# A hybrid decoder step: the recurrence's decays move into their own head's step, and four norms share one stretch of logarithms

## The reference

```python
h = rms_norm(x, norm_mix)
z = h @ w_in                            # 2048 -> 7 blocks of 8 heads x 128
q_a, k_a, v_a, q_r, f_r, i_r, g_r = split(z)
q_a = rotary(rms_norm(q_a, q_gain)); k_a = rotary(rms_norm(k_a, k_gain))
o_att = attend(q_a, k_a, v_a, lam)      # softmax of map 1 - lam * softmax of map 2
o_att = rms_norm(o_att, att_gain) * (1 - lam_init)
log_f = log(lb + (1 - lb) * sigmoid(f_r))          # the recurrence's decays
k_r = (1 - lb) * sigmoid(-f_r)
# per step t: S = exp(log_f[t]) * S + k_r[t] v[t];  o[t] = q_r[t] S
o_rnn, state = hgrn2_recurrence(q_r, k_r, i_r, log_f, state0)
o_rnn = rms_norm(o_rnn, rnn_gain) * silu(g_r)
x = x + concat([o_att, o_rnn]) @ w_out
```

## Time and profile before

| | us |
|---|---|
| median of 3 runs | 2925.33 (2924.01 to 2927.54) |
| the profiled execution | 2924.42 |
| its span (first to last record) | 2922.6 |
| around the span | 1.8 |
| a loop round by the windows, clock 1.00 | 113.41 |
| the same, clock 0.99 | 115.04 |

### The profile page before, as it was taken

The page is one execution under the profiler, slowest core; times in us unless marked ns, Lnnn a source line. Parts: engine busy times, 40 slices in busy tenths (PEclk is TensorE's granted clock), DMA queues, the critical chain, the costliest instruction groups (busy, mean ns, idle before and its releaser), DMA issues.

```text
span 2922.6 us, 53276 instructions
## 1 busy us (share of the span) xinstructions
PE 2859.9 (98%) x19979; PEld 2640.6 (90%) x19979; DVE 1502.3 (51%) x2459; ACT 1068.3 (37%) x1481; POOL 97.8 (3%) x75
## 2 busy tenths in 40 slices
PE   6999999999999999999999999999999999999998
PEld 5988888888888898999999999999999999998998
DVE  5455555554554645445554445544455444555454
ACT  4455455455464434222332222332223322234322
POOL 2011010010110100000000000000000000000000
PEclk8999999999999999999999999999999999999999
DMA  5333334333434532333233332333323333232332
GB/s 194 95 109 114 92 92 118 100 98 102 115 102 141 149 97 81 87 93 89 84 93 95 93 89 86 92 94 93 92 80 94 95 93 93 85 90 85 103 106 86
DMA packets 546619, 291.46 MB, mean 100 GB/s; under 512 B 15209, under 2 KB 537571, under 8 KB 546507
## 3 DMA queue, kind: packets, MB, share of 16 engines
q1 hardware_dynamic: 515482, 268.56, 31.5%
q10 hardware_dynamic: 31040, 21.46, 2.3%
HBM read 268.50 MB, written 21.63 MB: 99 GB/s over the span
## 4 chain that ended last, share of the span: by engine, by line
PE 92%; DVE 4%; ACT 2%; issue 2%; SPq 0%; DMA 0%; DVEq 0%; ACTq 0%
PE product L900 27%; PE product L904 14%; PE product L902 14%; PE product L901 14%; PE product L903 13%; PE scratch L707 2%; PE scratch L715 2%; PE scratch L756 1%; PE scratch L809 1%; DVE w_lo L1446 1%; ACT L1074 1%; DVE r_km L1659 1%; DVE act L1683 1%; PE scratch L795 1%; PE scratch L706 1%
## 5 line engine op out<-in xcount | busy, mean ns | idle before, releaser
L900 PE MATMUL product<-act,w_hi 128*128 128x512 f32 x2816 | 1150.9, 409 | 37.2 <-DVE act L1683 14.1
L1446 DVE TENSOR_TENSOR w_lo<-w_raw,w_hi 128x1024 fp32r<-128x1024 f32 (+1 forms) x496 | 607.8, 1226 | 556.7 <-ACT w_hi L1063 556.6
L1063 ACT ACTIVATE w_hi<-w_raw 128x1024 fp32r<-128x1024 f32 (+1 forms) x496 | 514.3, 1037 | 974.8 <-PE product L904 953.0
L904 PE MATMUL product<-act,w_lo 128*128 128x264 f32 x2816 | 807.8, 287 | 0.0
L902 PE MATMUL product<-act,w_hi 128*128 128x264 f32 x2816 | 803.2, 285 | 0.0
L901 PE MATMUL product<-act,w_hi 128*128 128x264 f32 x2816 | 801.9, 285 | 0.0
L903 PE MATMUL product<-act,w_lo 128*128 128x256 f32 x2816 | 794.2, 282 | 0.0
L902 PEld LDWEIGHTS product<-act,w_hi 128*128 128x128 f32 x2816 | 532.5, 189 | 128.6
L900 PEld LDWEIGHTS product<-act,w_hi 128*128 128x128 f32 x2816 | 535.3, 190 | 55.8 <-issue 23.8
L901 PEld LDWEIGHTS product<-act,w_hi 128*128 128x128 f32 x2816 | 535.2, 190 | 3.4 <-issue 1.9
L904 PEld LDWEIGHTS product<-act,w_lo 128*128 128x128 f32 x2816 | 534.4, 190 | 0.0
(11 more groups left out here) (249 smaller groups left out, 2459.4 us busy)
## 6 DMA issues: line engine op xcount, KB each, us to landing
w_raw<-in_w_in SPq DMA_DIRECT2D x112, 512.0 KB, 3.8
w_raw<-in_w_gate SPq DMA_DIRECT2D x88, 512.0 KB, 3.8
w_raw<-in_w_up SPq DMA_DIRECT2D x88, 512.0 KB, 3.8
w_raw<-in_w_down SPq DMA_DIRECT2D x64, 384.0 KB, 3.4
w_raw<-in_w_down SPq DMA_DIRECT2D x64, 320.0 KB, 3.2
w_raw<-in_w_out SPq DMA_DIRECT2D x32, 512.0 KB, 3.9
w_raw<-in_w_ple_gate SPq DMA_DIRECT2D x32, 384.0 KB, 3.4
k_pages<-in_cache_k SPq DMA_DIRECT2D x128, 64.0 KB, 2.8
```

Source lines behind the costliest of these rows:

```text
L900: pe.matmul(both, hi, x[:, k, :, 0:TA], start=begin, stop=False)
L904: mm = pe.matmul(far, lo, x[:, k, 1, TA:T], start=False, stop=end)
L1063: act.activation(w_hi[:, slot, 0:n, :], w_raw[:, slot, 0:n, :], ACT.Copy).then_inc(w_hi_ready, 1)
L1446: dve.tensor_tensor(flat(w_lo[:, slot, 0:n, :]), flat(w_raw[:, slot, 0:n, :]), flat(w_hi[:, slot, 0:n, :]).bitcast(F32), ALU.subtract).the ...
```

## The change

It rewrites the tables of slots. In the loop, the recurrence of head r moves up: `i_nat` 3 to 0, `kh_nat` 7 to 1, `upd` 9 to 2, `intra` 11 to 4, `rnn` 14 to 6, `s_upd` 16 to 7, `s_rnn` 18 to 8, `ssq_r` 20 to 11, and `ssq_a` of head r comes as a task of slot 11 of the next round, where it was slot 27 of its own. `ssq_q` moves from 6 to 10, `rot_q` from 8 to 13, `rot_k` from 12 to 14, `pages0` and `pages1` one slot earlier, `v_nat` from 14 to 15, `score0` from 15 to 16, `att_out` from 25 to 27. The tail has a table of its own.

```diff
 ATTENTION = {
-    6: ["ssq_q"], 8: ["rot_q"], 10: ["ssq_k"],
-    12: ["rot_k"], 13: ["pages0"], 14: ["pages1", "v_nat"], 15: ["k_nat", "score0"],
-    16: ["s_score"], 17: ["score1"], 18: ["w0"], 19: ["s_prob", "score2", "w1"],
-    21: ["score3"], 22: ["w2"], 24: ["w3", "s_out"], 25: ["s_turn", "att_out"], 27: ["ssq_a"],
+    10: ["ssq_q", "ssq_k"], 12: ["pages0"], 13: ["pages1", "rot_q"], 14: ["rot_k"], 15: ["v_nat", "k_nat"],
+    16: ["score0", "s_score"], 17: ["score1"], 18: ["w0"], 19: ["s_prob", "score2", "w1"],
+    21: ["score3"], 22: ["w2"], 24: ["w3", "s_out"], 25: ["s_turn"], 27: ["att_out"],
 }
 RECURRENCE = {
-    3: ["i_nat"], 7: ["kh_nat"], 9: ["upd"], 11: ["intra"], 14: ["rnn"], 16: ["s_upd"], 18: ["s_rnn"], 20: ["ssq_r"],
+    0: ["i_nat"], 1: ["kh_nat"], 2: ["upd"], 4: ["intra"], 6: ["rnn"], 7: ["s_upd"], 8: ["s_rnn"], 11: ["ssq_r", "ssq_a"],
+}
+RECURRENCE_ALONE = {
+    0: ["ssq_a", "i_nat", "kh_nat", "upd"], 4: ["intra"], 6: ["rnn"], 8: ["s_upd"], 10: ["s_rnn"], 12: ["ssq_r"],
 }
 HALVES = 2 * HEAD_CHUNKS
 
-K_PAGES_AT = {True: {10: range(NPG)}, False: {6: range(0, 6), 8: range(6, 11), 10: range(11, NPG)}}
+K_PAGES_AT = {True: {10: range(NPG)}, False: {4: range(0, 6), 6: range(6, 11), 8: range(11, NPG)}}
 V_PAGES_AT = {18: range(0, 6), 20: range(6, 11), 22: range(11, NPG)}
```

```diff
+        SUMS = {"ssq_q": (rr, DK, "rr_q"), "ssq_k": (sq, DK, "rr_k"), "ssq_a": (mix_a, P, "rr_a"), "ssq_r": (mix_r, P, "rr_r")}
+
+        def log_sum(name, it):
+
+            dst, count, _ = SUMS[name]
+            b = take(name, it)
+            func(two(dst[:, :]), m_wide(b), ACT.Ln, scale=1.0 / count, bias=K("eps")).then_inc(free[b], 1)
+
+        def inv_root(name, it):
+
+            dst, _, sig = SUMS[name]
+            act.wait_ge(*read(name, it))
+            func(dst[:, :], dst[:, :], ACT.Exp, scale=-0.5).then_inc(flag(sig), 1)
...
-                    func(sq[:, :], z_k[:, :], ACT.Square).then_inc(flag("sq_k"), 1)
-                if h is not None and s == 10:
+                    func(sq_k[:, :], z_k[:, :], ACT.Square).then_inc(flag("sq_k"), 1)
+                if h is not None and s == 12:
+
+                    beside = ["ssq_r", "ssq_a"] if r is not None else []
+                    for name in beside:
+                        log_sum(name, it)
+                    for name in ["ssq_q", "ssq_k"] + beside:
+                        inv_root(name, it)
+                if h is not None and s == 14:
```

```diff
+                if h is not None and s == 23:
+
+                    act.wait_ge(*evacuated("f", h))
                     func(r_k[:, :], z_f[:, :], ACT.Sigmoid, scale=-1.0)
                     func(z_f[:, :], z_f[:, :], ACT.Sigmoid).then_inc(flag("sig_f"), 1)
+                if r is not None and s == (23 if h is not None else 14):
+
+                    act.wait_ge(flag("r_normed"), r + 1)
                     act.wait_ge(*evacuated("g", r))
-                    func(r_g[:, :], z_g[:, :], ACT.Sigmoid).then_inc(flag("sig_g"), 1)
-                    act.wait_ge(flag("f_done"), r + 1)
+                    func(mix_r[:, :], z_g[:, :], ACT.Sigmoid).then_inc(flag("sig_g"), 1)
+                if h is not None and s == 23:
+                    act.wait_ge(flag("f_done"), h + 1)
                     func(r_kh[:, :], z_f[:, 0:SEQ], ACT.Ln).then_inc(flag("log_f"), 1)
-                if r is not None and s == 2:
-                    act.wait_ge(flag("b_left"), r + 1)
+                if h is not None and s == 25:
+                    act.wait_ge(flag("b_left"), h + 1)
                     func(r_kh[:, :], r_kh[:, :], ACT.Exp).then_inc(flag("exp_left"), 1)
-                    act.wait_ge(flag("b_mid"), r + 1)
+                    act.wait_ge(flag("b_mid"), h + 1)
                     func(r_qm[:, :], r_qm[:, :], ACT.Exp).then_inc(flag("exp_mid"), 1)
-                if r is not None and s == 4:
-                    act.wait_ge(flag("mid_b"), r * SUBS + SUBS)
+                if h is not None and s == 26:
+                    act.wait_ge(flag("mid_b"), h * SUBS + SUBS)
                     for i in range(SUBS):
                         func(r_km(i), r_km(i), ACT.Exp).then_inc(flag("exp_km"), 1)
                     func(r_e[:, :], r_b[:, :], ACT.Exp).then_inc(flag("exp_b"), 1)
@@ -1234,28 +1227,39 @@
...
+                if h is not None and s == 23:
+                    dve.wait_ge(flag("sig_f"), h + 1)
+                    dve.tensor_scalar(z_f[:, :], z_f[:, :], oml[:, bass.ds(h, 1)], lb[:, bass.ds(h, 1)], ALU.mult, ALU.add).then_inc(flag("f_done"), 1)
+                    dve.wait_ge(flag("f_done"), h + 1)
 
                     dve.tensor_copy(f_s[:, :], z_f[:, SEQ:T]).then_inc(flag("f_s_done"), 1)
-                    dve.tensor_scalar(r_k[:, :], r_k[:, :], oml[:, bass.ds(r, 1)], None, ALU.mult).then_inc(flag("r_k_done"), 1)
-                    dve.wait_ge(flag("sig_g"), r + 1)
-                    dve.tensor_tensor(z_g[:, :], z_g[:, :], r_g[:, :], ALU.mult).then_inc(flag("r_gate"), 1)
-
-                    dve.wait_ge(flag("log_f"), r + 1)
+                    dve.tensor_scalar(r_k[:, :], r_k[:, :], oml[:, bass.ds(h, 1)], None, ALU.mult).then_inc(flag("r_k_done"), 1)
+                if h is not None and s == 24:
+                    dve.wait_ge(flag("log_f"), h + 1)
                     for j in range(BLOCKS_T):
                         t = slice(j * P, (j + 1) * P)
                         scan = dve.tensor_tensor_scan(r_b[:, t], K("ones"), r_kh[:, t], 0.0, ALU.mult, ALU.add)
                     scan.then_inc(flag("scan_done"), 1)
-                    dve.wait_ge(flag("scan_done"), r + 1)
+                    dve.wait_ge(flag("scan_done"), h + 1)
                     rb = r_b[:, :].rearrange("p (c t) -> p c t", t=P)
                     dve.tensor_tensor(r_kh[:, :].rearrange("p (c t) -> p c t", t=P),
                                       rb[:, :, P - 1:P].broadcast_to([P, BLOCKS_T, P]), rb, ALU.subtract).then_inc(flag("b_left"), 1)
...
+            pool.wait_ge(flag("exp_left"), h + 1)
+            pool.wait_ge(flag("r_k_done"), h + 1)
             nc.gpsimd.tensor_tensor(r_kh[:, :], r_k[:, 0:SEQ], r_kh[:, :], ALU.mult).then_inc(flag("r_kh_done"), 1)
-            pool.wait_ge(flag("exp_mid"), r + 1)
-            nc.gpsimd.tensor_tensor(r_qm[:, :], z_r[:, 0:SEQ], r_qm[:, :], ALU.mult).then_inc(flag("r_qm_done"), 1)
             rk = r_k[:, 0:SEQ].rearrange("p (c t) -> p c t", t=P)
             for i in range(SUBS):
                 w = (i + 1) * SUB
-                pool.wait_ge(flag("exp_km"), r * SUBS + (i + 1))
+                pool.wait_ge(flag("exp_km"), h * SUBS + (i + 1))
                 t = nc.gpsimd.tensor_tensor(r_km(i), r_km(i), rk[:, :, 0:w], ALU.mult)
             t.then_inc(flag("r_km_done"), 1)
-            pool.wait_ge(flag("exp_b"), r + 1)
-            pool.wait_ge(flag("r_qm_done"), r + 1)
+            pool.wait_ge(flag("exp_mid"), h + 1)
+            pool.wait_ge(flag("exp_b"), h + 1)
+            pool.wait_ge(*evacuated("r", h))
+            nc.gpsimd.tensor_tensor(r_qm[:, :], z_r[:, 0:SEQ], r_qm[:, :], ALU.mult).then_inc(flag("r_qm_done"), 1)
+            pool.wait_ge(flag("r_qm_done"), h + 1)
             nc.gpsimd.tensor_tensor(r_qd, z_r[:, 0:SEQ], r_e[:, :], ALU.mult).then_inc(flag("r_qd_done"), 1)
```

```diff
+                if s == (10 if r is None else 4):
                     if r is None:
 
                         sp.wait_ge(flag("xT_written"), 16)
@@ -567,7 +571,8 @@
                         sp.wait_ge(flag("sq_sum_done"), SUM_EARLY)
                     else:
 
-                        sp.wait_ge(flag("mix_a_done"), h)
+                        sp.wait_ge(flag("sq_a"), h)
+                        sp.dma_start(s_state[:, :, :], a["state_rnn"][0, :, bass.ds(r, 1), :, :].rearrange("b h k v -> k (b h) v")).then_inc(flag("s_state_in"), 16)
...
-                dve.wait_ge(flag("rr_a"), n)
-                dve.scalar_tensor_tensor(mix_a[:, :], oT[:, :], gain_a[:, 0:1], rr[:, :], ALU.mult, ALU.mult).then_inc(flag("mix_a_done"), 1)
+            elif name == "norm_a":
+                dve.wait_ge(flag("rr_a"), m)
+                dve.scalar_tensor_tensor(mix_a[:, :], oT[:, :], gain_a[:, 0:1], mix_a[:, :], ALU.mult, ALU.mult).then_inc(flag("mix_a_done"), 1)
...
+            elif name == "gate_r":
+                dve.wait_ge(flag("sig_g"), m)
+                dve.tensor_tensor(z_g[:, :], z_g[:, :], mix_r[:, :], ALU.mult).then_inc(flag("r_gate"), 1)
                 dve.wait_ge(flag("r_gate"), m)
                 dve.tensor_tensor(mix_r[:, :], r_o[:, :], z_g[:, :], ALU.mult).then_inc(flag("mix_r_done"), 1)
...
+                if h is not None and s == 12:
+                    small("norm_q", it, h, r)
+                    small("norm_k", it, h, r)
+                if r is not None and s == 12:
+                    small("norm_r", it, h, r)
+                if r is not None and h is not None and s == 12:
+                    small("norm_a", it, h, r)
```

(20 more changed lines are left out.)

99 lines of the change are left out of this document (33 added, 66 removed).

## The result

| | before | after |
|---|---|---|
| median, us | 2925.33 (2924.01 to 2930.38) | 2944.07 (2941.03 to 2951.98) |
| profiled execution, us | 2924.42 | 2944.07 |
| its span | 2922.6 | 2942.3 |

The changed kernel is slower: ratio 1.0065, 95% interval 1.005 to 1.0081. The prediction said 2925.7 in a range of 2914 to 2934, so the time lies outside it, and the outcome that it called most likely, no change, did not come.

A forecast was written before the change was run, and what follows sets the result against it. PE, busy 98% of the span, was taken to bound the kernel. The terms -11.7 + 5.5 + 5.0 + 1.1 + 0.5 = +0.4 us gave 2924.8 for the profiled execution, a median of 2925.7 us, range 2914 to 2934.

The forecast's parts named there:

- no change: The forecast and its neighbours, within 0.2% (5.9 us) of the kernel before; chance 0.45.
- Part 1: Front of the round: PE's wait for `w_lo` at slot 4 goes in seven rounds, -11.7 us.
- Part 2: `score0` behind `low`: a new PE wait in all eight heads, +5.5 us, bounds 0 to 13.6.
- A: PE's wait at `score2` of slot 19 until `w0` is read from its scratch buffer, 0.7 us a head.
- Part 3: Decays ahead of chunk 13: a new PE wait in seven rounds, none in head 0, +5.0 us, bounds 0 and 13.3.
- B: PE's wait at slot 26 for the split of chunk 13 (`w_lo`), 0.7 us in each of seven rounds.
- Part 4: Norms at slot 12: ACT's and DVE's work is covered ahead of `rot_q`; cost 0, within about 1 us of showing.
- Part 5: Boundaries: loop entry +1.1 us, the return kept at 0.54 us seven times, the tail +0.5 us.
- The tail: After the loop: half the `act` wait and the `w_lo` wait go, `upd` waits about 3.5 us; +0.5 us, bounds -2 and +3.
- 0.54 is the return itself: At the loop's return: of PE's 0.79 us idle, 0.25 is the evacuation, 0.54 the return, kept seven times.
- Slow: Rival: B is 1.9 us instead of 0.7, ACT and DVE waiting for each other, 2934.1 us; chance 0.17 for B, 0.22 in all.
- Fast: Rival: A and B don't show, 2915.2 us, with one 2920.5; a covered return hole gives 3.8 us more; chance 0.33.

The follow-up runs named there:

- Experiment 2: The changed kernel with PE's seven rounds written out one after the other, other engines keeping their loops: 2928.84 us, ratio 1.0007.
- 4: The changed kernel with two more 128x260 matmuls, result unused, on PE behind `att_out` in all eight heads: 2949.12 us, ratio 1.0076.
- experiment 6: The kernel before with the seven rounds written out on PE alone: 2925.51 us, ratio 0.9998.
- 11: The kernel before with `intra` in two halves, behind the products of slots 11 and 12: 2926.28 us, ratio 1.0006.
- experiment 1: The changed kernel with `att_out` back at slot 25, so PE's round again ends with a product: 2936.16 us, ratio 1.0037.
- 3: The changed kernel with `intra`'s 32 small matmuls in two halves, behind the products of slots 4 and 5: 2939.11 us, ratio 1.0042.
- experiment 5: The changed kernel with PE's seven rounds written out and `intra` in two halves: 2920.79 us, ratio 0.9981 to the kernel before.
- 8: The changed kernel with only `v_nat` back at slot 14 and the gate behind slot 24's scan, its write at slot 25: 2936.7 us, ratio 1.0034.

## Why the prediction was wrong

**Right.** Part 1: slot 4's waits went, 11.7 us in all. Part 2: A predicted at 0.7 us a head, measured 0.76 (6.0 for 5.5). Part 3: B predicted at 0.7 in seven rounds and none in head 0, measured 0.72 (5.0 for 5.0). Its load is 1.28 us and nothing more; had it been the 2.66 of the Trainium skill, "ScalarE: Activation LUTs", "What ACT_TABLE_LOAD costs", B would have been 2.1. Part 4: no wait at `rot_q`. Part 5: the entry +1.1 for +1.1. The tail +1.2 for +0.5 is in its bounds, but partly by luck: the waits for `act` were to halve and went from 4.6 to 4.1 only, and the wait ahead of `upd` was to be 3.5 us and was 2.6. The terms named there (half of `act`, all of `w_lo`, 3.5) give +0.3 and not +0.5.

**Wrong, first: the return, in part 5.** "0.54 is the return itself, and I keep it seven times" took a remainder for a price (and there are six returns, not seven). The price is the branch, 3.3 to 3.9 us from its issue, and what PE has queued then hides it; the branch's row was in the trace of before and not read. The change put `att_out`, 20 short matmul instructions, last on PE's list, where four long ones of `ssq_a` behind a product had been, and the part that shows rose from between 0.8 and 1.2 us to between 1.5 and 2.1: +5.5 us. Of this, 4.8 is the shorter cover (0.8 us less at each return), and the rest is that the six branches took 0.7 us longer in all. Experiment 2 shows the branch as cause, and 4 that what is queued counts by its number of instructions: longer ones in the same places hide more, added ones push the branch's issue back. Experiments 6 and 11 show a second fault of the same step: before, that hole wasn't a cost of its own. It and slot 4's wait came to 2.5 us together, whatever their shares. The change took away the chain, and with it what hid the branch. The Trainium skill, "Runtime: NRT & Kernel Launch", "Instruction fetch mechanics", says that a taken branch whose target isn't among the current two pages waits until its instructions are fetched. The traces give 3.4 to 3.6 us (medians) for the branch and not 0.54. No row shows the fetch itself, and whether the second hole of experiment 1 belongs to it isn't shown.

**Wrong, second: the clock.** The prediction took slow stretches as drift, "it comes and goes without the work changing", 1.7 us either way. Here they follow the work for the greater part: seven in seven rounds, all behind `intra`, where before it was two, one of them behind `intra`. In the rounds that is 5 x 1.7 = 8.5 of +9.7 us, and in the tail two more, 3.4 us. It isn't one execution's bad luck: the mean granted clock is 0.984 to 0.988 in all five runs of the changed kernel, and 0.989 to 0.992 in 14 runs of the kernel before, timed with experiments 1 to 4. Experiments 3 and 5 show that thin stretches bring it, 32 small matmuls in a row or the return's hole: with `intra` in halves PE's busy time in the rounds falls from 789.3 to 782.1 us, and with the loop written out as well to 777.5, 11.9 us or seven times 1.7. Why it came in each round after the change and in one before, with the same 3.7 us of `intra` in both, isn't shown. Rounds of the change took 115.8 to 116.3 us each; experiments 2 and 8, with other lengths, had it in some rounds. That could point to the distance between such stretches, but it wasn't tested by changing the distance alone, and stays open.

**The rivals.** None named what happened. "Slow" had a bigger B for its mechanism, and B was as forecast. "Fast" had the hole at the return closing, and it opened. The waits that the sum added up came as forecast. Without the two misses, though, the change does better than its forecast of +0.4: written out and with halves (experiment 5) it is at 2920.8 us, where the kernel before written out (6) is at 2925.5. The 0.54 kept on both sides hid a gain: slot 4 and the return cost 2.5 us a round together, some 17 us in seven rounds, of which the sum counted 11.7. Part of the 4.7 us between the two kernels is the clock again, as the trace of experiment 6 has two slow stretches in its rounds and that of 5 none.

## What to carry over

At each loop's end on the engine that is the bound, read the branch's own duration and its issue time, and let that engine's list end with instructions that last long; or write the loop out. That gains only where nothing else holds the engine behind the jump: 15 us after the change, nothing before it. When a wait is removed, ask what else was hidden inside the same chain: here the jump back. Stretches of many small matmuls in a row can cost more than their own time through the clock of what follows; break them up among large ones, and count slow stretches, rather than take them for noise.
